# Weaving gate and raising projections into the attention loops of a hybrid encoder layer

## What is computed

```python
h = _rmsnorm(x, g_in)
proj = h @ w_in
y_a = _sliding_window_sink_attention(a_q, a_k, a_v, attn_sinks)
y_b = _dsa_sparse_attention(b_q, b_k, b_v, b_qi, b_ki, b_wi)
y_c = _memory_cross_attention(c_q, m_k, m_v)
ys = jnp.stack([y_a * silu(a_z), y_b * silu(b_z), y_c * silu(c_z)], axis=2)
u = jnp.einsum('bsnc,ncd->bsnd', ys, w_branch)
merged = jnp.sum(jax.nn.sigmoid(gates) * u, axis=2)
return x + merged @ w_out
```

## Time and profile before

| | us |
|---|---|
| median of three runs | 3220.39 (3218.98 to 3224.93) |
| the profiled execution | 3227.78 |
| its span | 3225.8 |

### The profile page before, as it was taken

One profiled execution on the slowest core, in us unless ns is written; L12 is line 12 of the kernel. 1 busy time (PEld: TensorE's weight loads), 2 busy tenths in 40 slices (PEclk: granted clock), 3 DMA queues, 4 the chain that ended last, 5 costly groups with the idle time before them and its releaser, 6 DMA issues.

```text
span 3225.8 us, 37577 instructions
## 1 busy us (share of the span) xinstructions
PE 2703.2 (84%) x13724; PEld 2257.2 (70%) x13724; DVE 1658.9 (51%) x3208; ACT 1426.6 (44%) x2598; POOL 607.9 (19%) x473
## 2 busy tenths in 40 slices
PE   5989896788898987988898987898889969667796
PEld 4777775666687876766787866786667758566685
DVE  4454544332553647323654657732386575666621
ACT  4454543342553624332753535543286455344521
POOL 4435262252111210111111210011101102000020
PEclk9999997989899999989999988998999989888998
DMA  5557283275353340254353340025433505100044
GB/s 167 188 165 254 89 271 91 83 251 169 131 169 119 124 138 1 98 177 134 120 168 119 119 136 7 1 78 185 136 131 123 162 21 192 52 1 1 1 136 158
DMA packets 169701, 392.28 MB, mean 122 GB/s; under 512 B 12848, under 2 KB 95792, under 8 KB 159536
## 3 DMA queue, kind: packets, MB, share of 16 engines
q1 hardware_dynamic: 169520, 389.89, 37.0%
HBM read 301.76 MB, written 88.08 MB: 121 GB/s over the span
## 4 chain that ended last, share of the span: by engine, by line
PE 54%; DVE 19%; ACT 10%; issue 8%; POOL 5%; DMA 3%; SPq 0%; ACTq 0%; DVEq 0%; POOLq 0%
PE PJ L684 39%; PE TR L572 6%; PE PJ L642 3%; DVE prob L1147 3%; DVE ptL L1185 3%; ACT prob L795 2%; ACT ptH L817 2%; POOL pairs L960 2%; ACT squared L774 1%; DVE ranks L1279 1%; DVE above L1226 1%; DMA xs<-in_x 1%; ACT prob L805 1%; DVE zs L1215 1%; PE SC L712 1%
## 5 line engine op out<-in xcount | busy, mean ns | idle before, releaser
L684 PE MATMUL PJ<-hH,pairs 128*128 128x512 f32 (+1 forms) x3584 | 1129.1, 391 | 12.2 <-POOL pairs L960 6.8
L684 PEld LDWEIGHTS PJ<-hH,pairs 128*128 128x128 f32 x3584 | 675.5, 190 | 155.8 <-POOL pairs L960 8.7
L684 PE MATMUL PJ<-hL,pairs 128*128 128x512 f32 (+2 forms) x1792 | 697.5, 389 | 0.0
L572 PE MATMUL TR<-identR,prob 128*128 128x128 f32 x1480 | 260.5, 303 | 206.5 <-ACT prob L795 156.1
L1185 DVE TENSOR_TENSOR ptL<-TR,ptH 128x512 fp32r<-128x512 f32 (+1 forms) x384 | 255.6, 669 | 266.0 <-ACT ptH L817 264.3
L684 PEld LDWEIGHTS PJ<-hL,pairs 128*128 128x128 f32 (+1 forms) x1792 | 340.0, 190 | 67.8
L1226 DVE TENSOR_SCALAR_CACHE_REDUCE above<-score,bits 128x256 uint8<-128x256 f32 (+10 forms) x280 | 348.1, 1243 | 54.3 <-POOL zs L996 45.1
L572 PEld LDWEIGHTS TR<-identR,prob 128*128 128x128 f32 x1480 | 192.0, 155 | 260.9 <-ACT prob L795 175.4
L828 ACT ACTIVATE signs<-score,bits 128x384 bf16<-128x384 f32 (+7 forms) x256 | 334.6, 1307 | 80.4 <-DVE bits L1239 73.1
L817 ACT ACTIVATE ptH<-TR 128x512 fp32r<-128x512 f32 (+1 forms) x384 | 219.2, 580 | 313.0 <-PE TR L572 312.6
L684 PE MATMUL PJ<-ysH,pairs 128*128 128x512 f32 x768 | 250.1, 397 | 26.2 <-ACT sg L883 16.8
(11 more groups left out here) (197 smaller groups left out, 4102.9 us busy)
## 6 DMA issues: line engine op xcount, KB each, us to landing
pairs<-w_split SPq DMA_DIRECT2D x444, 512.0 KB, 4.3
w_split<-pairs SPq DMA_DIRECT2D x74, 1024.0 KB, 4.8
raw<-in_w_in SPq DMA_DIRECT2D x106, 256.0 KB, 5.6
xs<-in_x SPq DMA_DIRECT2D x4, 2048.0 KB, 10.6
rows<-in_x SPq DMA_DIRECT2D x4, 2048.0 KB, 7.9
out<-rows SPq DMA_DIRECT2D x4, 2048.0 KB, 7.5
raw<-in_w_branch SPq DMA_DIRECT2D x24, 256.0 KB, 6.0
memkv<-mem_scratch SPq DMA_DIRECT2D x3, 2048.0 KB, 12.2
```

What stands on the lines that cost most here:

```text
L572: last = nc.tensor.transpose(bank, src, identR[0:k, 0:k].bitcast(F32))
L684: last = nc.tensor.matmul(o, lhs[:, k, :], rhs[:, row, 0:st.n_tok], start=(k == 0 and i == 0 and (up or half == 0)), stop=(k == BC - 1 and ...
```

## The change

All of `branch(0)`, `branch(2)` and the first two gates of `branch(1)` leave their own stages. `spread_over` cuts their units into single products and gives each place of an attention stage (and of the index stage) a number of them, which PE issues at the end of the place: two gates of C in attention C; ten units of C and two gates of A in attention A; ten units of A and two gates of B in attention B; two SiLU gates of C in the index stage. 24 products lie ahead of the first item in A and B and 12 after the last; in C and the index stage 12 ahead.

- The value products get a bank of their own (`PV`), `SC` becomes three banks of 512 columns, `ptH` and `ptL` have two places, not three. Only the next item is scored ahead in A and C. Masks and index copies go by 512 columns.
- ACT takes Tanh in place of Sigmoid (sigmoid(v) = (1 + tanh(v/2)) / 2; the factor one half is applied in `split_y` and `split_m`) and no longer copies `up`, `z` and `cq` results. DVE reads those banks itself (`emptied`); POOL only adds `up` results to `merged`.
- The search has 3 parts behind each C query and each of the first two SiLU gates of A, 1 per item in attention C, 2 behind every turned unit of A, 4 per item in attention A: 12, 4, 6, 12 and the last 30 of 64, in this order C queries, attention C, SiLU gates, turned units, attention A.
- `select` uses half-width flags with one more DVE instruction in phase 3.

```diff
-PER_UNIT, PER_PAIR, PER_ITEM = (2, 2, 2, 2), ((2, 2, 3), (2, 2, 3), (2, 1, 2), (1, 1, 2)), (0, 0, 0, 1)
+PER_UNIT, PER_C, PER_TURN, PER_A = 3, 1, 2, 4
 SEARCHED = 32 * 2
+PRODUCTS = 24
...
-def chunked(keys):
-
-    n = 1 if keys <= 1024 else 2
-    return [(c * (keys // n), keys // n) for c in range(n)]
+def chunked(keys, most=1024):
+
+    n = -(-keys // most)
+    size = -(-keys // (n * 32)) * 32
+    return [(c, min(size, keys - c)) for c in range(0, keys, size)]
...
+                if counting is not None:
+                    select_bits(counting, PER_TURN)
...
+    def spread_over(units, places, front=0, end=0):
+
+        total, at, to = PRODUCTS * len(units), 0, {}
+        for i, place in enumerate(places):
+            if i == 0:
+                upto = front
+            elif i == len(places) - 1:
+                upto = total
+            else:
+                upto = front + (total - front - end) * i // (len(places) - 2)
+            here = to.setdefault(place, [])
+            while at < upto:
+                un, first = units[at // PRODUCTS], at % PRODUCTS
+                last = min(PRODUCTS, first + upto - at)
+                here.append((un, first, last))
+                at += last - first
+        return to
...
+                for c, size in chunked(it.keys, T):
+                    it.chunks.append((e, c, size, take("s")))
+                    s_freed.append(event("dve_s") if branch == "b" else ("p_exp", n["e"] + len(it.chunks)))
+                for c, size in chunked(it.keys, 1024 if branch == "b" else T):
+                    it.exps.append((e, c, size, take("e")))
...
-            it.parts = counted(g, PER_ITEM[g]) if branch != "b" else None
+            it.parts = counted(g, {"a": PER_A, "c": PER_C}[branch]) if branch != "b" else None
...
+        places = [(-1, 0)] + [(it.i, j) for it in group.items for j in range(it.groups)] + [(len(items), 0)]
+        group.woven = spread_over(units, places, front, end)
...
+    def branch_units(which, g, first, last):
+
+        units = []
+        for at in range(first, last):
+            m, part = 2 * (at // 3), at % 3
+            if part < 2:
+                unit("gate", "w_in", GATES + which * D + (m + part) * P, m=m + part, into=units)
+            else:
+                unit("up", "w_branch", m * P, width=2 * P, moving="y", m=m, which=which, y=n["y"],
+                     first=(which == 2), g=g, into=units)
+        return units
+
+    def split_y():
+        steps.append(Step("split_y", y=take("y"), used=n["pv"]))
...
+        st.woven = spread_over(beside, range(-1, len(st.parts) + 1), PRODUCTS // 2)
         steps.append(st)
-        for role, src, col, more in gates_of(C_Z, g)[2:]:
+        for i in range(4):
+            queries = unit("cq", "w_in", C_Q + i * P, i=i)
+            select_bits(g, PER_UNIT)
+        attention("c", g, branch_units(2, g, 0, 2), 12, 0, queries.used)
+        split_y()
+        z_a = gates_of(A_Z, g)
+        for role, src, col, more in z_a[:2]:
             unit(role, src, col, **more)
-            select_bits(g, PER_UNIT[g])
-        for i in range(4):
-            unit("cq", "w_in", C_Q + i * P, i=i)
-            select_bits(g, PER_UNIT[g])
-        attention("c", g)
-        branch(2, g)
-        for role, src, col, more in gates_of(A_Z, g)[:2]:
-            unit(role, src, col, **more)
-        select_bits(g, PER_UNIT[g])
-        turned([("ak", "w_in", A_K, dict(g=g, y=n["y"])), ("av", "w_in", A_V, dict(g=g))]
-               + [("q", "w_in", A_Q + i * P, dict(g=g, i=i)) for i in range(4)], beside=gates_of(A_Z, g)[2:], counting=g if g > 1 else None)
-        attention("a", g)
-        branch(0, g)
-        for role, src, col, more in gates_of(B_Z, g)[:2]:
+            select_bits(g, PER_UNIT)
+        turned([("ak", "w_in", A_K, dict(g=g)), ("av", "w_in", A_V, dict(g=g))]
+               + [("q", "w_in", A_Q + i * P, dict(g=g, i=i)) for i in range(4)], beside=z_a[2:], counting=g)
+        attention("a", g, branch_units(2, g, 2, 12) + branch_units(0, g, 0, 2), 24, 12)
+        split_y()
+        z_b = gates_of(B_Z, g)
+        for role, src, col, more in z_b[:2]:
             unit(role, src, col, **more)
         select_bits(g, SEARCHED)
-        steps.append(Step("select", g=g, x=n["x"]))
-        turned([("q", "w_in", B_Q + i * P, dict(g=g, i=i)) for i in range(4)], beside=gates_of(B_Z, g)[2:])
-        attention("b", g)
-        branch(1, g)
-        steps.append(Step("load_rows", g=g, x=n["x"]))
+        steps.append(Step("select", g=g))
+        turned([("q", "w_in", B_Q + i * P, dict(g=g, i=i)) for i in range(4)], beside=z_b[2:])
+        attention("b", g, branch_units(0, g, 2, 12) + branch_units(1, g, 0, 2), 24, 12)
+        split_y()
+        for st in branch_units(1, g, 2, 12):
+            steps.append(st)
+            if st.role != "up":
+                continue
+            if st.m:
+
+                steps.append(Step("split_m", g=g, m=st.m - 2, x=st.evac - 1))
+            if st.m == 2 and g + 1 < NG:
+                prepare("x", g + 1)
+            elif st.m == 4 and g + 1 < NG:
...
+        PV = ctx.enter_context(nc.psum_tensor("PV", [P, T], F32))
-        SC = [ctx.enter_context(nc.psum_tensor(f"SC{i}", [P, 1024], F32)) for i in range(2)]
+        SC = [ctx.enter_context(nc.psum_tensor(f"SC{i}", [P, T], F32)) for i in range(3)]
...
+            def loads_after(st):
+                if once <= st.wt < split_end:
+                    store_pair(st.wt)
+                if st.wt + 2 < split_end:
+                    load_raw(st.wt + 2)
+                elif st.wt + 2 < len(units):
+                    load_pair(st.wt + 2)
...
-                    wait_bank(pe, pj_freed, it.u, "pj")
+                if j == 0 and it.pv:
+                    pe.wait_ge(S["dve_pv"], it.pv)
 
                 pe.wait_ge(S["tr_free"], it.tr + j + 1)
-                H, L = ptH[:, (it.p + j) % 3, :], ptL[:, (it.p + j) % 3, :]
-                bank = PJ[it.u % 2]
+                H, L = ptH[:, (it.p + j) % 2, :], ptL[:, (it.p + j) % 2, :]
+                bank = PV
...
+            def projected(st, first, last):
+
+                mH, mL = {"y": (ysH, ysL), "m": (mergedH, mergedL), "h": (hH, hL)}[st.moving]
+                up = st.role == "up"
+                if first == 0:
+                    if st.wt < split_end:
+                        pe.wait_ge(S["lo_ready"], st.wt + 1)
+                    if st.moving == "y":
+                        pe.wait_ge(S["y_lo"], st.y)
+                for n in range(first, last):
+                    half, k, i = n // 12, n % 12 // 3, n % 3
+                    row = k if up else half * BC + k
+                    if n % 12 == 0:
+                        if st.wt >= split_end:
+                            pe.wait_ge(pair_in[st.wt % 2][half], 16 * ((st.wt - split_end) // 2 + 1))
+                        if up or half == 0:
+                            wait_free(pe, pj_freed, st.u + half)
+                    if st.moving == "m" and st.m == 0 and i == 0:
+
+                        pe.wait_ge(S["m_lo"], st.g * KC + row + 1)
+                    vH, vL = hi_of(st)[:, half, k, :], lo_of(st)[:, half, k, :]
+                    lhs, rhs = ((vH, mH), (vH, mL), (vL, mH))[i]
+                    done = nc.tensor.matmul(PJ[(st.u + half * up) % 2][0:min(st.width, P), 0:st.n_tok], lhs, rhs[:, row, 0:st.n_tok],
+                                            start=(n % 12 == 0 and (up or half == 0)), stop=(n % 12 == 11 and (up or half == 1)))
+                    if n % 12 == 11:
+                        done.then_inc(S["tile_done" if half else "half_done"], 1)
+
+            def beside(st, place):
+                for un, first, last in st.woven.get(place, ()):
+                    projected(un, first, last)
...
+                        beside(st, n)
...
-                    ahead = 1 if branch == "b" else st.slots - 1
-                    for it in items[:ahead]:
-                        scores(it, branch, st.g)
+                    scores(items[0], branch, st.g)
+                    beside(st, (-1, 0))
...
-                            if branch == "b" and i + 1 < len(items):
+                            if i + 1 < len(items):
                                 scores(items[i + 1], branch, st.g, [n for n, at in enumerate(due(st, i)[0]) if at == j])
-                            elif branch != "b" and j == 0 and i + ahead < len(items):
-                                scores(items[i + ahead], branch, st.g)
+                            beside(st, (i, j))
...
-                if p >= 3:
-                    act.wait_ge(S["pv_done"], p - 2)
+                if p >= 2:
+                    act.wait_ge(S["pv_done"], p - 1)
                 cols = slice(0, width(it, j, branch))
-                nc.scalar.activation(ptH[:, p % 3, cols], TR[tr % 2][:, cols], ACT.Copy).then_inc(S["pt_hi"], 1)
+                nc.scalar.activation(ptH[:, p % 2, cols], TR[tr % 2][:, cols], ACT.Copy).then_inc(S["pt_hi"], 1)
...
```

(83 more changed lines are left out.)

523 lines of the change are left out of this document (226 added, 297 removed).

## The result

The changed kernel takes 3301.59 us (median of four runs, 3294.58 to 3305.36) where the kernel before takes 3219.68 in the same runs: a ratio of 1.0251, with a 95% interval of 1.0226 to 1.0276. The profiled span grew from 3225.8 to 3296.8 us, by 71.0, where a fall by 133 was forecast.

| us, all four groups | before, with the units that move in | forecast | measured | after |
|---|---|---|---|---|
| start, index projections, first two gates of C | 271.8 | 0 | +18.5 | 290.3 |
| index scores, two gates | 175.4 | -33 | -29.9 | 145.5 |
| C queries, attention C, two units | 260.4 | +1 | +2.3 | 262.7 |
| gates and projections of A | 276.4 | +38 | +56.6 | 333.0 |
| attention A, twelve units | 476.0 | -26 | +46.5 | 522.5 |

The account below looks back on a forecast made before the run. PE bounds stages of plain units; in the attention stages waits leave some 280 us of holes on PE. Terms sum to -133 on a span of 3225.8, giving 3093 and a forecast of 3087 us, range 2970 to 3185.

Parts of the forecast that it names:

- Attention B, -115 forecast: Attention B: woven units fill 130 us of PE's holes, less half of 30 us of extra masking; between -80 and -195.
- the sentence on `ptH`: Attention B: two places make ACT wait for a product issued about 0.7 us after the transposes; costed at nothing.
- The masks: Attention B: masking by 512 columns adds 128 instructions of 0.23 us, 30 us on DVE, half of it exposed.
- The absorption: Attention B: woven units fill PE's holes, 130 us taken of a ceiling of 197.
- The lengths that the prediction names as signs: Attention B, groups 0 to 3: near 150, 195, 245 and 340 us if the forecast is right.
- Attention A, -26 forecast: Attention A: 15 bits of search or PE's work set each group's length; 450 us against 214.9 + 261.2.
- rival D: Attention A: search bits stack on the woven attention, 710 us where 450 was taken; total 3347, chance 0.08.
- Rival C: Attention B: woven products delay the next exponential as much as they fill; -115 becomes +15, total 3217; chance 0.18.
- A's projections, +38 forecast: A's gates and projections: search parts behind the first two SiLU gates +5, two signs per turned unit +33.
- Index stages: Index stages: two SiLU gates join each, DVE and ACT set the length; 142 us against 131.6 + 43.6, -33.
- The hole ahead of branch B's first `up`: Start of branch B: PE waits for the split of y, about 4.5 us, four times, +18.
- The function table: ACT: Tanh stands between exponentials, most of 47 table loads (60 us) go or 185 us come; nothing taken for either.

Follow-up runs that it names:

- before_mask512: Kernel before, with DVE masking the scores of attention B in pieces of at most 512 columns: 3257.94 us.
- b_last_two_pv: Changed kernel with attention B's woven products at each item's last place, two value banks and two score banks: 3221.87 us.
- b_last: Changed kernel with attention B's woven products only at the last place of each item: 3271.28 us.
- c_plain_all: Changed kernel with third ptH/ptL place in attention B, its products at items' last places, two value and score banks, C's ten units plain with search behind: 3157.64 us.
- c_plain_pt3_last: c_plain_all with one value bank and three score banks, as in the changed kernel: 3178.97 us.
- b_front: Changed kernel with all twelve units of attention B ahead of its first item as plain units: 3471.40 us.

## Why the prediction was wrong, step by step

**Attention B, -115 forecast, -10 measured.** The step that failed is the sentence on `ptH`: that two places make ACT wait for a product which PE issues only 0.7 us after the transposes, and "I cost that at nothing". The 0.7 us was right (in the timeline above the products end 0.7 us after the transposes and ACT starts 0.8 after them), the nothing was not. I had asked what the wait costs ACT, which is idle more than half of the time; I hadn't asked what stands behind it. Behind it in one chain are `ptL`, the mask and the exponential that PE waits for at the item's end. One place less costs 87 us in the kernel before (52 of them in attention B); in the changed kernel the place given back to attention B alone takes 83 us off the total, 75.5 of them in that stage, where the loss of the change is 82. So this is shown by removing and by adding it. Without it the change would have been neither faster nor slower, so it alone doesn't save the forecast.

The masks were the right edit with the wrong share: half exposed in the prediction, all of it in before_mask512. That was measured on the kernel before, without woven units. The single value bank was not priced at all; alone it costs 7 us at most, but it caps what products at the item's end can fill (a second bank is worth 56 us in b_last_two_pv against b_last, and 35 with the ring of three, in c_plain_all against c_plain_pt3_last). The absorption itself was forecast at 130 us and was 146 with three places, 177 with two. It is the cost side that failed: 15 us forecast, 166 measured. With three places, the stage is 86 us below the sum of its parts, or 103 without the 17 us of the split, against the 115 forecast. Of the 166 us by which the bare attention grew, 106 are the ring, about 28 the masks, 16 the split ahead of branch B, which the forecast had in another row, and 7 the bank. Some 9 stay open, and the sum supposes that the terms are separate, which the three prices of the place say they are not quite. The lengths that the prediction names as signs, 150, 195, 245 and 340 us, sum to 930 and not to its 890. In group 0, where an item has one or two places and the ring of two costs nothing, the waits for exponentials fell from 35.8 to 7.5 us, by more than half as forecast, and the stage takes 125.6 us, less than its 150.

**Attention A, -26 forecast, +46 measured.** The forecast took the larger of PE's work and the chain of bits. Woven units and bits met on ACT and DVE instead, in an order that let each unit's bank wait behind 4 us of signs or counts. The step that failed is the larger of the two taken as the whole: I never wrote down the order of instructions on ACT and DVE within a place. With the order turned, the stage is 455.5 us where 450 was forecast, and that it is so close is in part luck. It is rival D in part: its mechanism (search exposed on a woven attention) with 72 of its 260 us. The bits themselves were priced too high (131 us for bare group 3, 111 measured), and even with the order turned group 3 takes 128.4 us, 17 more than the larger of 111 and PE's 103. Two errors of about the same size cancel there.

**Rival C** named the wrong carrier for the right outcome. Its text has the woven products delay the exponentials; they don't, as b_front shows, where the stage without them in the loop is 177 us longer. It does name "one place of `ptH` less", and put the whole case at 3217 with a chance of 0.18.

**A's projections, +38 forecast, +57 measured.** Length of the bits 36 us, as priced; the other 21 remain with bits of 64 keys. In group 0, 6 of them are there without any search. What they are is open.

One reading was off without effect. The holes on PE that the prediction puts at "some 280 us" are 197 us in attention B, 59 in attention A, 36 in the index stages and 38 in C, 330 in all. No term of its sum rests on the 280.

**The start, 0 forecast, +18.5 measured.** DVE now empties the memory keys' banks. PE waits once for that, while DVE scales the rows of x and makes the angles of the rotation, 11.5 us from 30.8 on; the row is from the changed kernel:

```profile
PE PJ L725 <- DVE memkv L1304: 9.1, 1, 9.1
```

I had taken DVE's new job of emptying at its own length and not looked at what is queued ahead of it in the stage outside the groups. The other 9 us are not explained.

**What held.** Index stages, -33 against -30; C, +1 against +2; B's selection, -16 against -14. The hole ahead of branch B's first `up` is as described, 17.0 us against the term of 18 (11.6 of them are put down to DVE's `ysL` below, group 0's 5.4 to issue). What else makes branch B longer was 6 in the forecast, for DVE's emptying of the `up` banks, and is 12.7; no run takes it apart. The function table cost nothing: 23 loads in place of 47, 6 of them at 96 gates and none in an attention stage, so a Tanh between exponentials needs none here. The Trainium skill (page "ScalarE: Activation LUTs", section "Table sets: the hidden batching unit") puts exp and tanh in one set, and the trace agrees.

```profile
L725 PE MATMUL PJ<-ysH,pairs 128*128 128x512 f32 x768 | 275.8, 422 | 67.7 <-ACT sg L912 46.7 <-DVE ysL L1527 11.6 <-issue 5.4
...
L912 ACT ACT_TABLE_LOAD x6 | 7.7, 1283 | 3.5 <-POOL merged L1036 3.4
```

The idea of the change was sound. With the ring, the value bank, the place of the products and the order of emptying put right, the same weaving gives 3090 us. That this is next to the 3087 of the forecast is coincidence: the terms are others, and some edits, like the index scores over four banks, were in no term of it.

## What to carry to other kernels

When a change takes a buffer to make room, price it by the chain that stands behind the waiting instruction, up to the wait that ends last, not by the idle time of the engine that waits. When work is woven into a loop, write down for one step of the loop the order on every engine, and put what gives a bank back to the busiest engine ahead of what only has to be done by the end. Filler helps where it stands directly ahead of the wait, if the bank behind it is free in time; spread evenly, most of it stands elsewhere (28 us of attention B with one value bank, 76 with two). And when a forecast and a result are compared row by row, see that a wait at a border is in the same row of both.
